# A two-layer hybrid trunk with eight experts: the expert stage in units of 1792 columns, light experts in plain float32

## What is computed

```python
for i in range(2):
    x = layer_norm(ALPHA * x + hybrid_mixer(x, ...))
    x = layer_norm(ALPHA * x + ffn(x))
# ffn of layer 0: dense SwiGLU, 2816 wide. ffn of layer 1:
logits = x @ w_router                        # 8 experts, top 2 per token, softmax of the two
for e in range(8):
    out += combine[:, e] * ((silu(x @ we_gate[e]) * (x @ we_up[e])) @ we_down[e])
```

## Time and profile before

| | us |
|---|---|
| median of 3 runs | 1277.31 |
| lowest and highest | 1277.2, 1278.26 |
| span of the profiled execution | 1276.0 |

### The profile page before, as it was taken

The page is one execution under the profiler, slowest core; times in us unless marked ns, Lnnn a source line. Parts: engine busy times, 40 slices in busy tenths (PEclk is TensorE's granted clock), DMA queues, the critical chain, the costliest instruction groups (busy, mean ns, idle before and its releaser), DMA issues.

```text
span 1276.0 us, 15815 instructions
## 1 busy us (share of the span) xinstructions
PE 1227.3 (96%) x6181; PEld 1053.5 (83%) x6181; DVE 1106.1 (87%) x861; ACT 933.7 (73%) x716; POOL 39.8 (3%) x57
## 2 busy tenths in 40 slices
PE   9999999999999999999999999999999999999886
PEld 8988888888989888888887877888787888887664
DVE  6978555568889999999999999999999899999887
ACT  5575444445868787888888888887988888788774
POOL 0100000001010000000000000000000000000100
PEclk9999999999999999999999999999999999999998
DMA  9947555537459999999999999999999999999993
GB/s 317 346 163 262 190 182 192 198 110 254 159 171 348 370 410 399 398 412 411 409 409 401 411 409 412 411 394 408 411 410 410 412 405 408 411 411 404 412 411 159
DMA packets 143556, 434.49 MB, mean 341 GB/s; under 512 B 8964, under 2 KB 50996, under 8 KB 131188
## 3 DMA queue, kind: packets, MB, share of 16 engines
q1 hardware_dynamic: 139936, 421.07, 85.8%
q0 software_dynamic: 3456, 12.32, 2.8%
q10 hardware_dynamic: 84, 0.02, 0.0%
HBM read 428.40 MB, written 4.98 MB: 340 GB/s over the span
## 4 chain that ended last, share of the span: by engine, by line
PE 61%; DVE 17%; DMA 15%; ACT 5%; issue 2%; SPq 0%; ACTq 0%; DVEq 0%
DVE w_lo L1032 14%; DMA raw<-in_we_down 8%; PE turn L1686 7%; PE turn L1688 7%; PE turn L1687 7%; PE accp L1686 5%; PE accp L1687 5%; PE accp L1688 5%; DMA raw<-in_we_gate 5%; PE turn L1798 4%; PE turn L1795 4%; ACT w_hi L669 4%; PE turn L1797 2%; PE turn L1796 2%; DMA raw<-in_we_up 2%
## 5 line engine op out<-in xcount | busy, mean ns | idle before, releaser
L1032 DVE TENSOR_TENSOR w_lo<-raw,w_hi 128x1792 fp32r<-128x1792 f32 (+3 forms) x447 | 895.8, 2039 | 96.8 <-ACT w_hi L669 91.5
L669 ACT CAST w_hi<-raw 128x1792 fp32r<-128x1792 f32 (+2 forms) x441 | 756.0, 1724 | 173.9 <-PE turn L1688 43.2
L2130 PE MATMUL turn<-w_hi,t_both 128*128 128x448 f32 x512 | 193.8, 379 | 16.0 <-DVE w_lo L1032 15.4
L2131 PE MATMUL turn<-w_lo,t_both 128*128 128x448 f32 x512 | 188.7, 369 | 0.0
L1686 PE MATMUL turn<-w_hi,a_hi 128*128 128x448 f32 x496 | 184.0, 371 | 0.0
L1688 PE MATMUL turn<-w_hi,a_lo 128*128 128x448 f32 x496 | 181.7, 366 | 0.0
L1687 PE MATMUL turn<-w_lo,a_hi 128*128 128x448 f32 x496 | 181.7, 366 | 0.0
L2130 PEld LDWEIGHTS turn<-w_hi,t_both 128*128 128x128 f32 x512 | 97.5, 190 | 36.6 <-issue 20.0
L2131 PEld LDWEIGHTS turn<-w_lo,t_both 128*128 128x128 f32 x512 | 97.4, 190 | 7.9 <-issue 0.2
L1686 PEld LDWEIGHTS turn<-w_hi,a_hi 128*128 128x128 f32 x496 | 93.1, 188 | 9.8
L1687 PEld LDWEIGHTS turn<-w_lo,a_hi 128*128 128x128 f32 x496 | 93.2, 188 | 8.4
(11 more groups left out here) (298 smaller groups left out, 1529.8 us busy)
## 6 DMA issues: line engine op xcount, KB each, us to landing
raw<-in_we_gate SPq DMA_DIRECT2D x128, 896.0 KB, 8.6
raw<-in_we_up SPq DMA_DIRECT2D x128, 896.0 KB, 9.2
raw<-in_we_down SPq DMA_DIRECT2D x96, 1024.0 KB, 9.6
raw<-in_w_in SPq DMA_DIRECT2D x18, 1024.0 KB, 9.0
raw<-in_we_down SPq DMA_DIRECT2D x32, 512.0 KB, 8.6
raw<-in_w_down SPq DMA_DIRECT2D x11, 1024.0 KB, 5.1
raw<-in_w_gate SPq DMA_DIRECT2D x10, 1024.0 KB, 5.3
raw<-in_w_up SPq DMA_DIRECT2D x10, 1024.0 KB, 5.4
```

The source lines that it names most:

```text
L669: nc.scalar.copy(w_hi[:, p % PARTS, 0:filled(p)], raw[:, p % RING, 0:filled(p)]).then_inc(hi_done, 1)
L1032: return nc.vector.tensor_tensor(out, whole, hi.bitcast(f32), ALU.subtract)
L2130: nc.tensor.matmul(to[:, c, :], few, wh[:, kk, c, :], start=(k == 0), stop=False)
L2131: last = nc.tensor.matmul(to[:, c, :], few, wl[:, kk, c, :], start=False, stop=(k == KD - 1))
```

## The change

Nothing changes before the expert stage, but for two things: the last reload of `ln_rows` moves, and `raw_more` takes memory of buffers that go. In the expert stage:

- **Units of 1792 columns**, 16 in all, in the order `"HH" + "LH" * 6 + "LL"`. A piece of gate or up is now one k-row of 128 x 1792, so each partition reads one run of 7168 bytes, where it was two of 3584. Bytes and matmuls of heavy units stay. Heavy downs are seven pieces of two blocks per unit; light ones eight, of two, two, two and one blocks, twice.
- **Gate and up in the same banks**: a heavy unit's gate fills all four banks of `turn`, and its up the same four after Silu has read them. The product stays in `silu_e`. Transposes go through bank 3 of `accp`, four blocks at a time, each waiting for the rounding of the four before.
- **Light experts unsplit**: their pieces skip ACT and DVE, and PE multiplies the raw buffer in float32 with 64 stationary columns of float32 tokens (`x_few`, `hT_few`). One half of the 1792 columns goes to PSUM partitions 0 to 63 and the other to 64 to 127, alternately; for the downs, one half of the output's columns each. `few_low`, `raise_low` and `add_low` go. A light piece holds its raw buffer until PE has used it.
- **Downs spread** over the gates and ups of the next unit (`order_in`), with the last two placed between gate and up, and after up.
- **Eight raw buffers**: `raw_more`, free from layer 1's mixer on, and `ln_rows`, from the layer norm on. The last reload of `ln_rows` is issued near the end, when its last piece has been used.
- **The end**: the last unit is light, so the last downs are float32 matmuls on raw pieces. Its rows are copied once and scattered by four float32 matmuls with 64 rows each. `add_rows` comes after all units on DVE.

```diff
-    ORDER = "HHH" + "LH" * 12 + "H" + "L" * QUARTERS
+    ORDER = "HH" + "LH" * 6 + "LL"
+    N_UNITS = len(ORDER)
+    DOWNS = {"H": 7, "L": 8}
...
+    def order_in(i):
+        if i == 0:
+            return "g" * KD + "u" * KD
+        order = ("gTgTdggdggSdggd" if light(i - 1) else "gTgTgTdgTggSdggd") + "uudVuudWuuduud"
...
-    WHOLE = {PLACE[piece] for piece in (("down", N_UNITS - 3, 1), ("down", N_UNITS - 2, 2))}
+    WHOLE = {PLACE[piece] for piece in PLACE if light(piece[1])}
+    MOE_SLOTS = [(MOE_AT + j) % RING for j in range(RING)] + [RING, RING + 1]
...
                     load(PLACE[which, i, pair],
-                         expert_rows(w, ORDER[i], k)[:, 2 * pair:2 * pair + 2, s * WIDE:(s + 1) * WIDE])
+                         expert_rows(w, ORDER[i], k)[:, pair:pair + 1, s * UNIT:(s + 1) * UNIT])
...
+            pool.wait_ge(piece_used, upto(LN_SLOT_LEFT))
+            reload_ln((ln2_g[1], ln2_b[1]))
...
+            def few_rows(i, which, k):
+                e, _ = expert_step(i)
+                if k == 0:
+                    if not which and not light(i - 1):
+                        up_left(i - 1, 0)
+                    else:
+                        up_left(i - 1, 1)
+                w = unsplit((up_piece if which else gate_piece)(i, k)).rearrange("p (h c f) -> p h c f", h=2, c=2)
+                for c in range(2):
+                    for h, rows in enumerate(HALVES):
+                        last = nc.tensor.matmul(half_banks[which][rows, c, :], x_few[:, e % 2, k, :], w[:, h, c, :],
+                                                start=(k == 0), stop=(k == KD - 1))
+                last.then_inc(piece_used, 1)
...
+            def few_down(i, pair):
+                _, s = expert_step(i)
+                half, quarter = divmod(pair, 4)
+                w = unsplit(down_piece(i, pair)).rearrange("p (j d) -> p j d", d=D)
+                hT = hT_few[:].rearrange("p (b h t) -> p b h t", h=2, t=FEW)
+                for j, block in enumerate(few_blocks(quarter)):
+                    for rows, cols in zip(HALVES, LAST):
+                        last = nc.tensor.matmul(few_sum[rows, :], hT[:, block, half, :], w[:, j, cols],
+                                                start=(s == 0 and pair == 0 and block == 0),
+                                                stop=(s == 1 and pair == 7 and block == FEW_BLOCKS - 1))
+                last.then_inc(piece_used, 1)
...
+            def many_rows(i, which, k):
+                e, _ = expert_step(i)
+                wh, wl = wide_columns(split((up_piece if which else gate_piece)(i, k)))
+                for c in range(4):
+                    if k == 0 and c % 2 == 0:
+                        if which:
+                            gate_left(i, c // 2)
+                        else:
+                            up_left(i - 1, c // 2)
+                    last = product(wide_banks[:, c, :], (xg_hi[e % 2][:, k, :], xg_lo[e % 2][:, k, :]),
+                                   (wh[:, c, :], wl[:, c, :]), k == 0, k == KD - 1)
+                last.then_inc(piece_used, 1)
```

More of the change, by code:

```diff
@@ L115, in fetch_at, with kept_in, visit_chunks @@
         return next((f for f in range(OTHERS) if i == (VISITS[visits_before(f) - 1][0] if f else 0)), None)
[L117 to L121, removed]
+    def kept_in(i):
+        return next((j for j, ek in enumerate(KEPT) if units(*ek)[-1] == i - 1), None)
+    def visit_chunks(j):
+        return sum(2 if FETCHED[f][0] == "H" else 1 for _, f in VISITS[:j])
@@ L123, in hybrid_trunk_kernel @@
     PLACE = {}
     for unit in range(N_UNITS):
[L125 to L128, removed]
+        rows_of_kind = {"g": iter(range(KD)), "u": iter(range(KD)), "d": iter(range(2 * KD))}
+        for c in order_in(unit):
+            if c in rows_of_kind:
+                which, of = {"g": ("gate", unit), "u": ("up", unit), "d": ("down", unit - 1)}[c]
+                PLACE[which, of, next(rows_of_kind[c])] = MOE_AT + len(PLACE)
@@ L129, in hybrid_trunk_kernel @@
+    for pair in range(DOWNS[ORDER[-1]]):
         PLACE["down", N_UNITS - 1, pair] = MOE_AT + len(PLACE)
+    MOE_PIECES = len(PLACE)
     IN_ORDER = sorted(PLACE, key=PLACE.get)
-    assert len(PLACE) == MOE_PIECES
+    assert MOE_PIECES == sum(2 * KD + DOWNS[kind] for kind in ORDER)
     def gate_piece(i, pair):
@@ L2052, in few_down_pair, with many_down @@
+            def many_down(i, pair):
+                _, s = expert_step(i)
+                wh, wl = split_rows(down_piece(i, pair))
+                for j in range(2):
+                    at = slice((2 * pair + j) * P, (2 * pair + j + 1) * P)
                     for c in range(2):
                         cols = slice(c * BANK, (c + 1) * BANK)
-                        nc.tensor.matmul(accp[:, 2 + c, :], hT_packed[:, block, :], wh[:, j, cols],
-                                         start=(first and block == 0), stop=False)
@@ L2056, in few_down_pair @@
[L2056 to L2068 removed]
+                        last = product(accp[:, c, :], (hT_hi[:, at], hT_lo[:, at]), (wh[:, j, cols], wl[:, j, cols]),
+                                       s == 0 and pair == 0 and j == 0, s == 1 and pair == BLOCKS // 2 - 1 and j == 1)
@@ L2083, in down_pair @@
-            def down_pair(pair, w, first, last_one):
-                wh, wl = [a[:, 0:len(blocks_of(pair)) * D].rearrange("p (j d) -> p j d", d=D) for a in w]
-                for j, block in enumerate(blocks_of(pair)):
-                    at = slice(block * P, (block + 1) * P)
-                    for c in range(2):
-                        cols = slice(c * BANK, (c + 1) * BANK)
-                        last = product(accp[:, c, :], [a[:, at] for a in (hT_hi, hT_lo)],
-                                       (wh[:, j, cols], wl[:, j, cols]), first and block == 0,
-                                       last_one and block == BLOCKS - 1)
-                return last
+                wh, wl = wide_columns(split((up_piece if which else gate_piece)(i, k)))
@@ L2279, in _ @@
             for i in range(N_UNITS):
+                gates, ups, downs, turned = 0, 0, 0, 0
                 if i == 0:
                     first_gate()
-                else:
-                    before_gate(i)
-                    for pair in range(4):
-                        if pair == 1:
-                            turn_h(i - 1)
-                        rows_pair(i, 0, pair)
-                    turned_left(i - 1)
-                pairs = {"u": 0, "d": 0}
-                kinds = mixed(i)
@@ L2306, in _ @@
+            for c in range(chunks(N_UNITS - 1)):
+                turn_h(N_UNITS - 1, c)
+            for pair in range(DOWNS[ORDER[-1]]):
+                down(N_UNITS - 1, pair)
             last_scatter()
```

720 lines of the change are left out of this document (345 added, 375 removed).

## The result

| | before | after |
|---|---|---|
| median | 1277.26 us | 1353.8 us (1353.23 to 1355.19) |
| ratio, 95% interval | 1 | 1.0598 [1.0583, 1.0612] |
| span of the profiled execution | 1276.0 us | 1351.5 us |

A forecast was written before the change was run, and what follows sets the result against it. The prediction took the weight transfer as the bound from about 456 us, PE before. Head 9 + bytes 12.5 - reload 2.6 + tail 5.3 = 24.2 us off span 1276.0: 1251.8, median 1253; range 1244 to 1285.

The forecast's parts named there:

- Does PE stay under the transfer?: Middle of the expert stage: 98 us of PE work per light and heavy pair, under 105 us of transfer.
- new waits: Transposes and rounding in the middle: PE finds the bank free; a late piece would hold PE, with 7 us room per pair.
- The head: Start of the stage: PE bounds until 477 us, and the transfer gets 4.2 MB further ahead, taken as 9 us gained.
- The room: PE's slack per pair in the middle of the stage: 7 us.
- rival 2: Light slots: PE's clock falls to half in idle gaps; seven drops in each of eight slots give 1284; chance 0.06.
- Column halves (rival 1): Light units: forecast has halves together, 36 us; the rival has them one after another, 72 us, 1461 us total; chance 0.16.
- Bytes: Gate and up transfers after 477 us: runs of 7168 bytes land in 2.19 us instead of 2.25, 12.5 us gained.
- Rival 3: Gate and up transfers: length of run gives nothing, 1266; chance 0.10.
- Reload of `ln_rows`: Last reload now falls into the full transfer stretch: 1.05 MB at 408 GB/s, 2.6 us lost.
- Tail: After the last landing: 16.8 us to the end instead of 22.1, 5.3 us gained.
- The sum: Whole kernel: 24.2 us less than a span of 1276.0, so span 1251.8 and median 1253; chance 0.68.
- The price list: PE's costs per matmul: heavy products of 448 columns 0.207 us, of 512 0.226; whole float32 products 0.75 and 0.86.

The follow-up runs named there:

- Experiments 1 to 4: Changed kernel, cumulative edits: last heavy down's low part before the multiply, 1319.26 us; light slots split three ahead, 1286.55; one at last light up, 1272.05; heavy three ahead, 1265.07.
- experiment 7: Fastest version (1265.07 us) with 12 of the 32 products of each light gate or up left out; every transfer, split and wait kept: 1265.56 us.
- Experiment 10: Fastest version (1265.07 us) with six raw buffers instead of eight: 1326.78 us.
- experiment 4: Changed kernel with light and heavy pieces split three ahead, one ahead at the last light up; also called the fast version: 1265.07 us.
- experiment 1: Changed kernel; in light slots DVE splits the heavy down after the last up before its multiply, no longer after: 1319.26 us.

## Why the prediction was wrong

The step that failed is **"Does PE stay under the transfer?"**, together with the paragraph on new waits that stood behind it. It has three faults, and a fourth stands in **"The head"**.

1. *It summed work per pair and took the sum for a schedule.* "ACT and DVE have 23 split pieces per pair instead of 46 ... so they fall far below" is right as a sum (both under half busy after) and said nothing of when each split may start. That ACT's rounding and its splits share one queue was seen, but in one direction only: rounding behind a split that waits for a landing. There the prediction also took ACT to split the piece after the next, and in light slots it is only the next. The other direction cost the time: the split behind the rounding, whose transposes PE makes at the last moment, and DVE's split behind a multiply that waits for the last up. The two numbers that fix this, `p + 1` and `p + 0` in light units, stood in the code of the change and were not followed. Experiments 1 to 4 give it its size: 34.5 for the last up, 47.2 for the light slots (1319.26 to 1272.05), 7.0 for the heavy ones, 88.7 us of the 100.8 between forecast and result. The other 12.1 are, by the estimate below, mostly the head's (fault 4).
2. *The room was priced too large.* PE's work in a pair of the fast version, by the distances between starts at full clock, is 104.2 us and not 98: heavy gates and ups 40.3 (39.7), light ones 25.7 (24), heavy downs 20.6 (19.0), light downs 13.4 (12), transposes 3.1 (3), tokens and choice 1.1 (not counted). Left are 1 to 3 us of room in place of 7. PE was busy 107.6 us per pair in the changed kernel (121.3 less 13.7 idle), and the other 3.4 are its clock: matmuls of 512 from 664.84 on stand 0.43 apart after the wait of 4.31, where 0.23 is usual. This is what rival 2 named, but as a consequence of the waits. With them gone the mean clock is 1.00. PE's work costs nothing once the splits are early (experiment 7).
3. *The buffers were counted without the lead.* "Four in flight suffice today, and six remain" holds only while nothing has to have landed early. Experiment 10 prices the two extra buffers at 61.7 us, where the prediction had used them for 4.5 us at the head.
4. *The lead at the head didn't come.* The transfer was to be 4.2 MB ahead of the kernel before at 477 us, taken as 9 us. The windows of 318 to 477 us, of the kernel before and then of the version of experiment 4:

```profile
318.00:477.00 159.00, 158.05 (x870) 141.07 (x869) 145.61 (x184) 119.98 (x103) 5.76 (x8) 1.00 0.78 289
```
```profile
318.00:477.00 159.00, 154.03 (x841) 138.47 (x840) 132.56 (x147) 111.59 (x96) 5.12 (x6) 0.99 0.75 277
```

   289 and 277 GB/s over 159 us are 1.9 MB less instead of more. 1.05 MB of them are the reload of `ln_rows`, which comes later now, so the weights are 0.9 MB behind. The working let the transfer run at 408 GB/s in a stretch in which, by its own words, PE was the bound and so set when buffers came free. In the changed kernel 384 to 480 us show 344 GB/s, and from 384 to 477 SP waits 76.0 us for low parts that free a raw buffer.

The other steps:

- **Column halves (rival 1)**: the choice of 36 us was right. A gate piece takes 1.61 us with both halves and 3.12 with one (half of 3.23 and of 6.23), and 1.5 or 3.0 were forecast. The surcharge of 7% on 24 us is part of fault 2. The Trainium skill (TensorEngine Tiling (Array Packing), Overview, Theoretical Speedup) has up to twofold for 64 columns or fewer. The runs agree, with 1.93.
- **Bytes**: 12.5 us forecast, with 0 and 15 as ends; 15.4 measured with the order mended. Rival 3 is out. By the least transfer for line rate in the Trainium skill (DMA: Bandwidth & Descriptors, Specifications), 512 bytes, nothing was left to gain. The measurement differs and decides: between runs of 3584 and 7168 bytes there are still 2%.
- **Head**: first light product at 482.1 for 477; the lead of the transfer is fault 4.
- **Reload of `ln_rows`**: no run separates its 2.6 us.
- **Tail**: 16.1 us for 16.8. The terms that the prediction lists add up to 17.3 and not 16.8. Its own range, 1246 to 1269, is of spans, while 1253 is a median.
- **The sum, had the order been right**: the version of experiment 4 has a span of 1262.8 for 1251.8: 4.2 at the head (481.2), 6 x 2.15 in the pairs, and 6.1 less at the end. Fault 4 is worth about these 11.0 us. Where the transfer is the bound, missing bytes are missing time: the 9 us that were put down didn't come, and 0.9 MB behind are 2 us at 415 GB/s (an estimate from the windows). How they spread over the pairs, and whether something else keeps a pair at 107.15, is left open: PE is idle for 34 of 760 us there, and the first slot runs at 389 GB/s, so the ring isn't full at once.

The price list in the prediction gave PE's order of magnitude, and 12.6 us less than the kernel before (1265.07 for 1277.71), with 24.2 forecast, was there to be had. The kernel that was to be predicted hid it behind two small constants.

## What to carry to other kernels

When a change makes two engines half idle, don't stop at their sums. For each kind of piece write down behind which instruction of its own engine it stands, who releases that one, and how much work the consumer has in between; here 4.4 us of split stood against 2.4 us of PE's work. Look-ahead and ring depth have to be chosen together (pieces split ahead + in use + in flight), and an instruction that waits for the consumer's newest result should stand behind the splits of the next pieces, unless it frees something the consumer needs at once, like the multiply at a last up.

## What the runs showed of the hardware

- Float32 products with 64 stationary columns, sent alternately to output partitions 0 to 63 and 64 to 127, take 1.61 us per gate piece of four products (3.23 for the 16 instructions of two pieces), and 3.12 (6.23) when all go to one half. Sending two of one half after each other costs next to nothing (3.28 for 3.23), so strict alternation isn't needed.
- Reading gates and ups, two thirds of the bytes, in runs of 7168 bytes instead of 3584 moved 415 in place of 406 GB/s in all, at a full DMA share in both.
- TensorE's granted clock fell from 2.4 to 1.2 GHz behind single waits, with the engine full before and after. A window of the changed kernel behind the wait of 4.31 us:

```profile
664.30:667.20 2.90, 2.90 (x7) 2.32 (x8) 2.90 (x2) 0.00 (x0) 0.00 (x0) 0.50 1.00 416
```

  The length of the wait alone doesn't tell whether it falls. Seven waits of the changed kernel between 480 and 1240 us are 2.56 or 2.57 us long. Behind two of them (ending at 491.73 and 617.29) the matmuls of 512 columns kept their distance of 0.23 us, and behind the other five they went to 0.43, at once or within three of them. Behind a wait of 3.55 us in the kernel of experiment 1 (ending at 541.66) the clock stayed full. One of the five:

```profile
859.11 0.76 PE L1734 MATMUL accp<-w_hi,t_both 128*128 128x512 f32 x1 [2.57 <-DVE w_lo L1105]
859.67 0.63 PE L1735 MATMUL accp<-w_lo,t_both 128*128 128x512 f32 x1
860.10 0.63 PE L1736 MATMUL accp<-w_hi,t_both 128*128 128x512 f32 x1
```

  In the version of experiment 4 the longest wait between 480 and 1240 us, 2.39 us, was followed by half clock too, though the mean of the whole stretch rounds to 1.00:

```profile
1203.60:1206.60 3.00, 2.95 (x8) 1.11 (x10) 0.00 (x0) 0.00 (x0) 0.00 (x0) 0.50 1.01 419
```
